# VectorE's modulation sums with 32x32 transpositions in place and folding products on TensorE

## The chip, the cores and the metric

The kernel runs on one core of one Trainium2 chip. The metric is the time of one execution on the device, in microseconds (us), taken as the median of several runs. Every matmul is in fp32 or in the fp32r form.

## What is computed

One layer of a hybrid diffusion backbone, for 128 context tokens and 128 latent tokens, width 2048. The shift, scale and gate vectors of three sublayers come from a modulation product, one row for the context and one for the latent tokens:

```
def modulation(cond, ada_w, ada_b):
    mod = jax.nn.silu(cond) @ ada_w + ada_b          # ada_w: 2048 x (9 * 2048)
    return jnp.split(mod[..., None, :], N_MOD, axis=-1)

xc = ffn_sublayer(xc, sh1, sc1, g1, ...)             # x + 0.5 * gate * swiglu(modulate(rms_norm(x)))
mq, mk, mv, ... = mixer_inputs(xc, sh2, sc2, ...)    # one 2048-wide input projection
...                                                  # mLSTM scan and windowed attention
xc = xc + g2 * merge_branches(...)                   # ends with the output projection w_out
xc = ffn_sublayer(xc, sh3, sc3, g3, ...)
```

The same layer runs on both groups of tokens, with the same weights. The change concerns how parts of `silu(cond) @ ada_w` are summed.

## The kernel before

**Units.** Both groups of tokens (2 x 128) share every weight. A weight tile of 256 x 512 is one unit: ScalarE rounds it (`w_hi`, L1354), VectorE makes the remainder (`w_lo`, L1810), and TensorE runs twelve matmuls of 512 columns on it (L702 to L704, three for each of two row blocks and two groups). `split(us + k + AHEAD)` prepares a unit three ahead of the one that TensorE is to work on; there are four slots for split weights, and ScalarE waits until TensorE has done the unit four before. There are 728 units in all. Each engine has a program of its own, written out by hand; semaphores tie them.

**The stages.** First FFN (a prologue, a loop over eight chunks of 512 hidden columns, and a last chunk), the input projection, the mLSTM and attention part, a merge, the output projection (`U_OUT`, four column chunks n of eight units k), the second FFN (in its loop two chunks a pass).

**The modulation.** The 36 chunks of 512 modulation columns are computed beside the units, in two ways. Half of them are products on TensorE. The other 18 are summed on VectorE: `products` (L1865) multiplies a 128x512 tile of `ada_w` by one scalar per partition and adds it to an accumulator of 2 x 512 columns per partition (`vec_acc`, `vec_m`, `vec_o`), 32 such steps for one chunk. What is left is a sum over the 128 partitions, and the result must lie with the columns on the partitions (`adacols`). For that, `vec_T` transposes the accumulator on TensorE, eight blocks of 128x128 into two PSUM banks (L648), and `sum_cols` reduces them on VectorE (L1838, 128x1024 to 128x8) and adds the bias (L1841).

**Where they stand.** In the first FFN's loop `vec_T` is called between units 6 and 7 of the eight output units (counted from 0), followed by the selection products (`ada_sel`, L656) and the transpositions of h (`h_transposes`, L779). L779 writes banks 4 and 5, and waits for the accumulation (L2015, semaphore `acc_done`) that VectorE makes at k = 5. In the last chunk `vec_T` comes after the first six units of the output part; before it, `ada_T` (L663) waits for VectorE's copy `ada_blk` (L1826). In the input projection it comes after the unit v = 11 of the second sixteen, in the output projection after units (n, k) = (1, 1) twice, (2, 1) and (3, 2), and in the second FFN after the second output unit of each odd chunk (`between`). The function `late_cols` calls `sum_cols` for these late chunks.

**Memory.** `cst` holds constants (identity, selection matrix, two triangles, two masks, cosines and sines); all tiles placed behind it in the same sequence, `hT_hi` and `hT_lo` among them, follow its width. The tiles from `cst` up to the slot of the accumulator `acc` take 8192 bytes per partition.

## Time and profile before

| | us |
|---|---|
| median of three runs | 2237.07 (2235.94 to 2237.38) |
| the profiled execution | 2237.59 |
| its span | 2235.6 |
| TensorE busy (PE) | 2207.9, 99% |
| VectorE busy (DVE) | 1607.7, 72% |
| ScalarE busy (ACT) | 937.0, 42% |

The times inside the profile are counted from the start of the span. Rows of a timeline give the start, the duration, the engine, the line, the operation with its operands and the number of instructions merged into the row; a bracket at the end tells how long the engine was idle before it, and what ended that. Durations of neighbouring matmuls overlap, so what a block of them costs is read from start to start. The stages lie at about 190 to 835 us (the loop and the last chunk of the first FFN), from 870 (input projection), from 1400 to 1495 (output projection) and from there on (second FFN).

### The profile page before, as it was taken

What the parts mean: (1) busy time and instruction counts of PE and PEld (TensorE: products, weight loads), DVE (VectorE), ACT (ScalarE), POOL (GpSimd) and SP (SyncE); (2) the same over time, 40 slices, a digit from 0 to 9 for tenths busy, and PEclk for the clock granted to TensorE, in tenths of its full rate; (3) what the DMA queues carried; (4) which work ended last, traced back from release to release, by engine and by line L of the source; (5) the groups of instructions that cost most, each with busy time, mean ns of one, the idle gap of its engine ahead of it and who ended that gap; (6) DMA issues with size and microseconds to landing.
All of it is one profiled execution on the core that took longest, in us unless ns stands there. A gap on an engine that the chain in (4) does not pass through costs nothing.

```text
span 2235.6 us, 28405 instructions
## 1 busy us (share of the span) xinstructions
PE 2207.9 (99%) x10498; PEld 1773.5 (79%) x10498; DVE 1607.7 (72%) x1859; ACT 937.0 (42%) x1100; POOL 64.5 (3%) x55
## 2 busy tenths in 40 slices
PE   6999999999999999999999999999999999999999
PEld 3567787878778778888888888888888888888887
DVE  3447888878887879746867888885567676776756
ACT  3333333333333336445544344454434444344443
POOL 0001000000000000000600000100000000000000
PEclk9999999999999999999999999999999999999999
DMA  9998898778887886644536776746675757557563
GB/s 361 385 367 292 287 322 300 278 277 291 315 283 281 281 271 208 217 161 160 190 109 234 260 258 234 270 157 207 224 241 190 263 188 262 188 188 262 188 226 131
DMA packets 273333, 548.15 MB, mean 245 GB/s; under 512 B 9014, under 2 KB 9418, under 8 KB 273008
## 3 DMA queue, kind: packets, MB, share of 16 engines
q1 hardware_dynamic: 212676, 423.69, 55.5%
q10 hardware_dynamic: 57484, 113.47, 14.1%
q0 software_dynamic: 3104, 10.05, 1.6%
q8 instruction: 46, 0.75, 0.1%
q14 instruction: 23, 0.19, 0.0%
HBM read 543.71 MB, written 3.46 MB: 245 GB/s over the span
## 4 chain that ended last, share of the span: by engine, by line
PE 96%; DVE 1%; DMA 1%; ACT 1%; issue 0%; SPq 0%; ACTq 0%
PE ps L702 30%; PE ps L704 29%; PE ps L703 29%; PE ps L639 1%; PE ps L624 1%; DMA ada_w_sb<-in_ada_w 1%; PE ps L779 1%; PE ps L648 1%; PE ps L689 0%; PE ps L1108 0%; PE ps L1176 0%; PE ps L656 0%; PE ps L1184 0%; DVE xm L1925 0%; DVE w_lo L1810 0%
## 5 line engine op out<-in xcount | busy, mean ns | idle before, releaser
L1354 ACT CAST w_hi<-raw_w 128x1024 fp32r<-128x1024 f32 x728 | 765.6, 1054 | 1171.3 <-PE ps L704 1128.7
L1810 DVE TENSOR_TENSOR w_lo<-raw_w,w_hi 128x1024 fp32r<-128x1024 f32 x728 | 897.4, 1236 | 433.5 <-ACT w_hi L1354 429.4
L702 PE MATMUL ps<-w_hi,xT_hi 128*128 128x512 f32 x2080 | 822.0, 395 | 5.8 <-DVE xT_lo L1893 4.5
L704 PE MATMUL ps<-w_hi,xT_lo 128*128 128x512 f32 x2080 | 811.1, 390 | 0.0
L703 PE MATMUL ps<-w_lo,xT_hi 128*128 128x512 f32 x2080 | 810.6, 390 | 0.0
L702 PEld LDWEIGHTS ps<-w_hi,xT_hi 128*128 128x128 f32 x2080 | 391.2, 188 | 111.0 <-issue 25.0
L704 PEld LDWEIGHTS ps<-w_hi,xT_lo 128*128 128x128 f32 x2080 | 390.9, 188 | 83.2
L703 PEld LDWEIGHTS ps<-w_lo,xT_hi 128*128 128x128 f32 x2080 | 391.3, 188 | 78.4
L1865 DVE SCALAR_TENSOR_TENSOR vec_acc<-ada_w_sb,ctile,vec_acc 128x512 f32<-128x512 f32 x420 | 299.2, 746 | 0.0
L702 PE MATMUL ps<-w_hi,hT_hi 128*128 128x512 f32 x704 | 276.2, 392 | 0.0
L704 PE MATMUL ps<-w_hi,hT_lo 128*128 128x512 f32 x704 | 274.2, 390 | 0.0
L703 PE MATMUL ps<-w_lo,hT_hi 128*128 128x512 f32 x704 | 273.9, 389 | 0.0
L704 PEld LDWEIGHTS ps<-w_hi,hT_lo 128*128 128x128 f32 x704 | 132.1, 188 | 27.7
L702 PEld LDWEIGHTS ps<-w_hi,hT_hi 128*128 128x128 f32 x704 | 132.2, 188 | 26.9 <-issue 0.2
L703 PEld LDWEIGHTS ps<-w_lo,hT_hi 128*128 128x128 f32 x704 | 132.3, 188 | 26.8
L2015 DVE TENSOR_TENSOR acc<-acc,ps 128x1024 f32<-128x1024 f32 x72 | 88.0, 1222 | 48.5 <-PE ps L704 48.5
L702 PE MATMUL ps<-w_hi,hcT_hi 128*128 128x512 f32 x128 | 50.1, 391 | 0.0
L704 PE MATMUL ps<-w_hi,hcT_lo 128*128 128x512 f32 x128 | 49.9, 390 | 0.0
L703 PE MATMUL ps<-w_lo,hcT_hi 128*128 128x512 f32 x128 | 49.8, 389 | 0.0
L1865 DVE SCALAR_TENSOR_TENSOR vec_m<-ada_m,ctile,vec_m 128x512 f32<-128x512 f32 x60 | 43.2, 746 | 0.0
L533 POOL DMA_DIRECT2D gate_dram<-gate_rows x3 | 1.6, 535 | 1414.8 <-DVE gate_rows L1821 1414.8
L1817 DVE TENSOR_TENSOR ada_rows_sb<-ps,ada_bias 128x512 f32<-128x512 f32 x18 | 12.2, 678 | 39.1 <-PE ps L624 39.1
(281 smaller groups left out, 1059.2 us busy)
## 6 DMA issues: line engine op xcount, KB each, us to landing
raw_w<-in_ffn_wi SPq DMA_DIRECT2D x176, 1024.0 KB, 5.2
ada_w_sb<-in_ada_w ACTq DMA_DIRECT2D x96, 1024.0 KB, 8.3
raw_w<-in_ffn_wo SPq DMA_DIRECT2D x88, 1024.0 KB, 5.3
raw_w<-in_w_in SPq DMA_DIRECT2D x68, 1024.0 KB, 5.4
ada_w_sb<-in_ada_w SPq DMA_DIRECT2D x30, 1024.0 KB, 13.0
raw_w<-in_w_out SPq DMA_DIRECT2D x16, 1024.0 KB, 5.3
ada_m<-in_ada_w ACTq DMA_DIRECT2D x12, 1024.0 KB, 5.2
raw_w<-in_w_proj_m SPq DMA_DIRECT2D x8, 1024.0 KB, 5.2
```

The lines of the kernel that those rows point to most:

```text
L624: mm = pe.matmul(ps[32 * j:32 * j + 32, 6, :], ctile[:, 4 * q + j, :], w[:, q, j, :], start=(q == 0), stop=(q == 3))
L639: mm = pe.matmul(ps[32 * j:32 * j + 32, 6, :], ctile[:, 4 * q + j, :], ada_w_sb[:, t, j, :], start=(q == 0), stop=(q == 3))
L648: mm = pe.transpose(ps[:, bank + g, b * P:(b + 1) * P], vec[:, g, b * P:(b + 1) * P], ident)
L702: pe.matmul(out, a_hi, w_hi[:, slot, kk, :], start=(first and kk == 0), stop=False)
L703: pe.matmul(out, a_hi, w_lo[:, slot, kk, :], start=False, stop=False)
L704: mm = pe.matmul(out, a_lo, w_hi[:, slot, kk, :], start=False, stop=(last and kk == 1))
L779: mm = pe.transpose(ps[:, 4 + b // 2, (b % 2) * TOK + g * P:(b % 2) * TOK + (g + 1) * P], h[:, g, b * P:(b + 1) * P], ident)
L1354: act.copy(w_hi[:, us % SPL, :, :], raw_w[:, slot, 2 * half:2 * half + 2, :]).then_inc(hi_ready, 1)
L1810: dve.tensor_tensor(w_lo[:, us % SPL, :, :], raw_w[:, slot, 2 * half:2 * half + 2, :], w_hi[:, us % SPL, :, :].bitcast(F32), ALU.subtract) ...
L1817: dve.tensor_tensor(ada_rows_sb[:], ps[:, 6, :], ada_bias[:, par, :], ALU.add).then_inc(ada_rows_done, 1)
L1865: ins = dve.scalar_tensor_tensor(acc[:, g, :], w, scale, acc[:, g, :], ALU.mult, ALU.add)
L2015: dve.tensor_tensor(acc[:, :, c], acc[:, :, c], ps[:, banks:banks + 2, :], ALU.add).then_inc(acc_done, 1)
```

## The change

The 18 sums over partitions are made differently. VectorE transposes the 128x1024 accumulator in place in blocks of 32x32 (`vec_fold`), waits for that, and reduces each run of 32 elements, which leaves 128x32 partial sums in `folded`. TensorE then adds the four groups of 32 partitions with a folding matrix: four products of 32 stationary and 8 moving columns (`vec_sum`) in place of eight transpositions. VectorE adds the bias straight from PSUM; the reduction after TensorE's part is gone. `vec_fold` is placed by hand: in the first FFN's loop at k = 5 of the output units, in its last chunk at e = 1, in the input projection at v = 26, in the output projection at (n, k) = (1, 0), (1, 2), (2, 0) and (3, 1), in the second FFN at k = 14 of the odd chunk's sixteen input units. The second sum of the output projection moves from (1, 1) to (1, 3) on TensorE. The masks are no longer constants: VectorE makes them from the triangles at v = 10, where ScalarE copied them; the constants grow by the folding matrix and lose the masks (816 to 592 columns), and the first part of them, which is loaded first, grows from 160 to 192 columns.

```diff
@@ -106,8 +106,8 @@
 
 
 
-C_ID, C_SEL, C_TRI, C_MASK, C_COS, C_SIN, C_TWO = 0, 128, 160, 416, 672, 736, 800
-C_W = 816
+C_ID, C_SEL, C_FOLD, C_TRI, C_COS, C_SIN, C_TWO = 0, 128, 160, 192, 448, 512, 576
+C_W = 592
 
 
 def shape_constants():
@@ -117,8 +117,7 @@
     c[:, C_ID:C_ID + P] = s == t
     c[:, C_TRI:C_TRI + P] = s <= t
     c[:, C_TRI + P:C_TRI + 2 * P] = s >= t
-    c[:, C_MASK:C_MASK + P] = np.where(s > t, 1e30, 0)
-    c[:, C_MASK + P:C_MASK + 2 * P] = np.where(s < t, 1e30, 0)
+    c[:, C_FOLD:C_FOLD + 32] = s % 32 == np.arange(32)[None, :]
     nf = HD // 4
     inv = np.float32(10000.0) ** (-np.arange(nf, dtype=np.float32) / np.float32(nf))
     for half, pos in enumerate((np.arange(P) // GRID_W, np.arange(P) % GRID_W)):
@@ -252,6 +251,7 @@
         row_sum = place("row_sum", [P, 2 * AH])
         neg_max = place("neg_max", [P, 2 * AH])
         biascol = place("biascol", [P, 4 * (NMOD * NCH - VCH2)])
+        folded = small[:, 16:48]
         hstat = small[:, 16:48].rearrange("p (a c) -> p a c", a=4)
 
         num = place("num", [P, NC, MV + 1], at=SCR)
@@ -297,7 +297,8 @@
         cols_ps, cond_silu, zeroed = sem("cols_ps"), sem("cond_silu"), sem("zeroed")
         ada_landed, bias_landed = sems("ada_landed", 4), sems("bias_landed", 2)
         ada_x_landed = sems("ada_x_landed", 2)
-        one_ready, mac_done, acc_T_done, acc_summed = sem("one_ready"), sem("mac_done"), sem("acc_T_done"), sem("acc_summed")
+        one_ready, mac_done = sem("one_ready"), sem("mac_done")
+        vec_turned, vec_folded, vec_summed = sem("vec_turned"), sem("vec_folded"), sem("vec_summed")
         ada_m_landed = sems("ada_m_landed", 2)
         ada_used, ada_rows_done = sem("ada_used"), sem("ada_rows_done")
         ada_sel_done, ada_cols_done = sem("ada_sel_done"), sem("ada_cols_done")
@@ -639,14 +640,14 @@
                     mm = pe.matmul(ps[32 * j:32 * j + 32, 6, :], ctile[:, 4 * q + j, :], ada_w_sb[:, t, j, :], start=(q == 0), stop=(q == 3))
                 mm.then_inc(ada_used, 1)
 
-            def vec_T(c, vec, done, bank):
+            def vec_sum(c, n, bank):
 
                 pe.wait_ge(ada_cols_done, c)
-                pe.wait_ge(mac_done, done)
-                for g in range(GROUPS):
-                    for b in range(4):
-                        mm = pe.transpose(ps[:, bank + g, b * P:(b + 1) * P], vec[:, g, b * P:(b + 1) * P], ident)
-                mm.then_inc(acc_T_done, 1)
+                pe.wait_ge(vec_folded, n)
+                for b in range(4):
+                    mm = pe.matmul(ps[32 * b:32 * b + 32, bank, 0:4 * GROUPS], cst[:, C_FOLD:C_FOLD + 32],
+                                   folded.rearrange("p (x b) -> p b x", b=4)[:, b, :], start=True, stop=True)
+                mm.then_inc(vec_summed, 1)
 
             def ada_sel(p, c):
 
@@ -909,7 +910,7 @@
                         if f == 0 and m == 1:
                             ada_T(i + 7)
                         if f == 0 and m == 2:
-                            vec_T(2 * i + 6, vec_acc, VEC_Z, 6)
+                            vec_sum(2 * i + 6, i - 1, 6)
                     if f == 0:
                         pe.wait_ge(ada_cols_done, VCH2)
                     for g in range(GROUPS):
@@ -934,7 +935,7 @@
                     with pe.Fori(2, FCH - 1) as i:
                         def sums():
                             pe.wait_ge(silu_done, i + 1)
-                            vec_T(2 * i + 5, vec_acc, (i - 1) * VEC, 0)
+                            vec_sum(2 * i + 5, i - 1, 0)
                             pe.wait_ge(gate_rows_ready, i - 1)
                             ada_sel(i + 7, 2 * i + 5)
 
@@ -943,7 +944,7 @@
                     with pe.Fori(1, 5) as t:
                         def between(n):
                             if n == 0:
-                                vec_T(t + 4 * G3 - 1, vec_acc, t * VEC + VEC_F2, 6)
+                                vec_sum(t + 4 * G3 - 1, t + FCH + 3, 6)
 
                         step(2 * t)
                         step(2 * t + 1, between)
@@ -1042,7 +1043,7 @@
                 if v == 7:
                     gate_rows_T()
                 if v == 11:
-                    vec_T(VCH2, vec_acc, VEC_M, 6)
+                    vec_sum(VCH2, FCH - 1, 6)
                 if v == 10:
                     scan_T()
                 if v == 12:
@@ -1086,7 +1087,7 @@
                 else:
                     pe.wait_ge(decays_ready, i - 1)
                 if i == 0:
-                    pe.wait_ge(masks_ready, 1)
+                    pe.wait_ge(masks_ready, 2)
                 for hd in range(MH):
                     out = ps[:, 4 + i % 2, hd * P:(hd + 1) * P]
                     pe.matmul(out, ident_r[:], mask_r[:, d, :], start=True, stop=False)
@@ -1323,12 +1324,13 @@
                         pe.wait_ge(mixT_lo_ready, min(k + 2, 8))
                     unit(U_OUT + 8 * n + k, 0, xT_hi, xT_lo, 2 * k, 2 * (n % 2), k == 0, k == 7)
                     if n == 1 and k == 1:
-                        vec_T(VCH, vec_m[0], VEC_O, 4)
-                        vec_T(VCH, vec_m[1], VEC_O, 6)
+                        vec_sum(VCH, FCH, 4)
+                    if n == 1 and k == 3:
+                        vec_sum(VCH + 1, FCH + 1, 6)
                     if n == 2 and k == 1:
-                        vec_T(VCH + 2, vec_m[2], VEC_O, 4)
+                        vec_sum(VCH + 2, FCH + 2, 4)
                     if n == 3 and k == 2:
-                        vec_T(VCH + 3, vec_o, VEC_F2, 4)
+                        vec_sum(VCH + 3, FCH + 3, 4)
             for g in range(GROUPS):
                 for k in range(4, 8):
                     mm = unit(U_OUT + 24 + k, 0, xT_hi, xT_lo, 2 * k, 2, False, k == 7, groups=(g,))
@@ -1628,8 +1630,7 @@
                     ada_tile(VCH, v - 1, v - 1)
                 if v == 10:
                     act.wait_ge(consts_landed, 16)
-                    act.copy(ident_r[:], cst[:, C_ID:C_ID + P])
-                    act.copy(mask_r[:].rearrange("p d t -> p (d t)"), cst[:, C_MASK:C_MASK + 2 * P]).then_inc(masks_ready, 1)
+                    act.copy(ident_r[:], cst[:, C_ID:C_ID + P]).then_inc(masks_ready, 1)
                 if v == 18:
                     act.wait_ge(absf_ready, 1)
                     chain(act.activation(exp_negm[:], absf[:], ACT.Exp, scale=-1.0))
@@ -1831,14 +1832,19 @@
                 dve.tensor_copy(adacols[:, bass.ds(4 * at, 4), :],
                                 ps[:, 7, P:2 * P].rearrange("p (b x) -> p b x", x=32)[:, :, 0:GROUPS]).then_inc(ada_cols_done, 1)
 
+            def vec_fold(n, vec, done):
+
+                dve.wait_ge(mac_done, done)
+                flat = vec[:].rearrange("p g n -> p (g n)")
+                dve.transpose(flat, flat).then_inc(vec_turned, 1)
+                dve.wait_ge(vec_turned, n)
+                dve.tensor_reduce(folded, flat.rearrange("p (x k) -> p x k", k=32), AX.X, ALU.add).then_inc(vec_folded, 1)
+
             def sum_cols(c, n, bank, bias, done=None):
 
                 dve.wait_ge(ada_cols_done, c if done is None else done)
-                dve.wait_ge(acc_T_done, n)
-                dve.tensor_reduce(small[:, 48:56], ps[:, bank:bank + 2, :].rearrange("p g (b k) -> p (g b) k", k=P), AX.X, ALU.add
-                                  ).then_inc(acc_summed, 1)
-                dve.wait_ge(acc_summed, n)
-                dve.tensor_tensor(adacols[:, bass.ds(4 * c, 4), :], small[:, 48:56].rearrange("p (g b) -> p b g", g=GROUPS),
+                dve.wait_ge(vec_summed, n)
+                dve.tensor_tensor(adacols[:, bass.ds(4 * c, 4), :], ps[:, bank, 0:4 * GROUPS].rearrange("p (g b) -> p b g", g=GROUPS),
                                   bias.unsqueeze(2).to_broadcast([P, 4, GROUPS]),
                                   ALU.add).then_inc(ada_cols_done, 1)
 
@@ -1982,6 +1988,8 @@
                             d_products(i, k)
                         if g3:
                             g3_products(g3[1], g3[2], g3[0] + k)
+                            if g3[0] and k == 14:
+                                vec_fold(g3[1] - 4 * G3 + FCH + 4, vec_acc, g3[2] + VEC)
                         if k == 15:
                             dve.wait_ge(units_done, us + ux + 16)
                             dve.wait_ge(silu_done, FCH * f + i + 1)
@@ -1992,6 +2000,8 @@
                 def ffn_out(j, us, ux, ada=None, g3=None):
 
                     for k in range(8):
+                        if ada is not None and k == 5:
+                            vec_fold(j, vec_acc, j * VEC)
                         if ada is not None and k == 7:
                             sum_cols(2 * j + 7, j, 0, biascol1[:, bass.ds(8 * j - 8, 4)])
                         split(us + k + AHEAD, ux)
@@ -2048,6 +2058,8 @@
                                 gates_copy((G1,), i - 1)
                                 ada_rows(i + 7, 1, 16 * i + 48)
                                 d_products(i, 16)
+                            if e == 1:
+                                vec_fold(i - 1, vec_acc, VEC_Z)
                             if e == 3:
                                 ada_blk(i + 7)
                             if e == 4:
@@ -2240,6 +2252,12 @@
                 if v:
                     split(U_IN + v + AHEAD, 0)
                 products(MACS_Z, 0, VCH2, VEC_Z, v)
+                if v == 10:
+                    dve.wait_ge(consts_landed, 16)
+                    dve.tensor_scalar(mask_r[:].rearrange("p d t -> p (d t)"), cst[:, C_TRI:C_TRI + 2 * P], -1e30, 1e30,
+                                      ALU.mult, ALU.add).then_inc(masks_ready, 1)
+                if v == 26:
+                    vec_fold(FCH - 1, vec_acc, VEC_M)
                 if v == 28:
                     late_cols(VCH2, 6, VCH)
                 if v == 16:
@@ -2483,10 +2501,19 @@
                     split(U_OUT + 8 * n + k + AHEAD, 0)
                     products(MACS_O, 0, VCH2, VEC_O, 8 * n + k, [ada_w_sb[:, q % 2, :, :] for q in range(4)], [ada_landed[q % 2] for q in range(4)],
                              [(400, 400)[q % 2] + 16 * (1 + q // 2) for q in range(4)], vec_o)
-                    if n == 1 and k in (2, 3):
-                        late_cols(VCH - 2 + k, 2 * k, VCH - 1 + k)
+                    if n == 1 and k == 0:
+                        vec_fold(FCH, vec_m[0], VEC_O)
+                    if n == 1 and k == 2:
+                        late_cols(VCH, 4, VCH + 1)
+                        vec_fold(FCH + 1, vec_m[1], VEC_O)
+                    if n == 1 and k == 4:
+                        late_cols(VCH + 1, 6, VCH + 2)
+                    if n == 2 and k == 0:
+                        vec_fold(FCH + 2, vec_m[2], VEC_O)
                     if n == 2 and k == 2:
                         late_cols(VCH + 2, 4, VCH + 3)
+                    if n == 3 and k == 1:
+                        vec_fold(FCH + 3, vec_o, VEC_F2)
                     if n == 3 and k == 3:
                         late_cols(VCH + 3, 4, VCH2)
                 c = slice(n * CH, (n + 1) * CH)
```

## Rows read from the trace of the kernel before

**Rows 1.** The page: busy lines, the chain that ended last, the costliest groups.
```profile
PE 2207.9 (99%) x10498; PEld 1773.5 (79%) x10498; DVE 1607.7 (72%) x1859; ACT 937.0 (42%) x1100; POOL 64.5 (3%) x55
...
PE 96%; DVE 1%; DMA 1%; ACT 1%; issue 0%; SPq 0%; ACTq 0%
...
L702 PE MATMUL ps<-w_hi,xT_hi 128*128 128x512 f32 x2080 | 822.0, 395 | 5.8 <-DVE xT_lo L1893 4.5
...
L702 PE MATMUL ps<-w_hi,hT_hi 128*128 128x512 f32 x704 | 276.2, 392 | 0.0
```

**Rows 2.** Timeline of TensorE, output projection, n = 3: transpositions standing alone.
```profile
1476.85 0.39 PE L704 MATMUL ps<-w_hi,xT_lo 128*128 128x512 f32 x1
1477.08 1.03 PE L648 MATMUL ps<-cst,vec_o 128*128 128x128 f32 x8
1477.87 0.48 PE L702 MATMUL ps<-w_hi,xT_hi 128*128 128x512 f32 x1
1478.18 0.40 PE L703 MATMUL ps<-w_lo,xT_hi 128*128 128x512 f32 x1
```

**Rows 3.** Timeline of TensorE, first FFN's loop, one of eight passes.
```profile
261.02 1.03 PE L648 MATMUL ps<-cst,vec_acc 128*128 128x128 f32 x8
...
262.34 1.09 PE L779 MATMUL ps<-cst,h 128*128 128x128 f32 x8
```

**Rows 4.** Timeline of TensorE, three stretches: small products.
```profile
205.24 1.92 PE L639 MATMUL ps<-ada_w_sb,ctile 128*32 128x512 f32 x16
...
823.58 0.43 PE L656 MATMUL ps<-ada_rows_sb,cst 128*32 128x128 f32 x8
823.94 0.50 PE L702 MATMUL ps<-w_hi,hT_hi 128*128 128x512 f32 x1
824.28 0.40 PE L703 MATMUL ps<-w_lo,hT_hi 128*128 128x512 f32 x1
...
933.29 0.61 PE L1007 MATMUL ps<-lf,cst 128*128 128x8 f32 x4
933.76 0.48 PE L702 MATMUL ps<-w_hi,xT_hi 128*128 128x512 f32 x1
```

**Rows 5.** Groups of VectorE by line and shape: busy, mean ns | idle before.
```profile
L1838 DVE TENSOR_REDUCE small<-ps 128x8 f32<-128x1024 f32 x18 | 22.0, 1222 | 9.7 <-PE ps L648 9.7
...
L1862 DVE TENSOR_SCALAR vec_acc<-ada_w_sb,ctile 128x512 f32<-128x512 f32 x28 | 12.6, 481 | 0.0
...
L1841 DVE TENSOR_TENSOR adacols<-small,biascol 128x8 f32 x12 | 2.0, 168 | 3.1 <-DVE small L1838 3.1
...
L1841 DVE TENSOR_TENSOR adacols<-small,biascol 128x8 f32<-128x8 f32 x6 | 1.0, 167 | 0.2
```

**Rows 6.** Timeline of all engines, last chunk of the first FFN.
```profile
822.65 2.47 DVE L1810 TENSOR_TENSOR w_lo<-raw_w,w_hi 128x1024 fp32r<-128x1024 f32 x2
...
829.27 0.28 DVE L1826 COPY ada_rows_sb<-ps 128x128 f32<-128x128 f32 x1
...
829.61 0.33 PE L663 MATMUL ps<-cst,ada_rows_sb 128*128 128x128 f32 x1
```

**Rows 7.** Timeline of VectorE, first FFN's loop, the pass of rows 3.
```profile
255.42 1.41 DVE L1865 SCALAR_TENSOR_TENSOR vec_acc<-ada_w_sb,ctile,vec_acc 128x512 f32<-128x512 f32 x2
...
258.59 1.22 DVE L2015 TENSOR_TENSOR acc<-acc,ps 128x1024 f32<-128x1024 f32 x1 [0.49 <-PE ps L704]
```

**Rows 8.** Timeline of all engines, input projection.
```profile
952.59 2.35 DVE L1810 TENSOR_TENSOR w_lo<-raw_w,w_hi 128x1024 fp32r<-128x1024 f32 x2
...
954.00 1.04 PE L648 MATMUL ps<-cst,vec_acc 128*128 128x128 f32 x8
```

**Rows 9.** Timeline of all engines, output projection, n = 1 and n = 3.
```profile
1427.32 0.74 DVE L1865 SCALAR_TENSOR_TENSOR vec_o<-ada_w_sb,ctile,vec_o 128x512 f32<-128x512 f32 x1
...
1428.15 1.04 PE L648 MATMUL ps<-cst,vec_acc 128*128 128x128 f32 x8
...
1474.86 2.35 DVE L1810 TENSOR_TENSOR w_lo<-raw_w,w_hi 128x1024 fp32r<-128x1024 f32 x2
```

## The prediction

> **What bounds the kernel now.** I read the page's busy lines first: TensorE is busy for 99% of the span [rows 1], and the chain of work that ended last is TensorE for 96% of it [rows 1]. The waits of TensorE come next: its largest group of matmuls, 2080 of them, has 5.8 us of idle time ahead of it in the whole span, 4.5 of them put down to VectorE's xT_lo [rows 1]. So a microsecond taken off TensorE's queue comes off the time, and a wait put into that queue is paid in full. Then I read the timelines around the places the change touches, to see what TensorE's own work costs there and how early VectorE, which is busy 72% of the time, gets to the same place.
>
> **TensorE: what the transpositions cost now.** There are 18 vector sums of eight transpositions, 144 in all: eight in the loop of the first FFN, and ten that stand alone (one after that loop, one in the input projection, four in the output projection, four in the second FFN). The page's means (0.27 us for one) overlap each other, so I go from start to start.
> - Alone: the eight start at 1477.08 and the following matmul at 1477.87; that matmul then takes 0.31 us to the next start, against 0.23 in the steady stream (1476.85 to 1477.08) [rows 2]. So 0.79 + 0.08 = 0.87 us each.
> - In the loop: they start at 261.02, and behind them and the four selection products (L656) the eight transpositions of h (L779) at 262.34 [rows 3]. So 1.32 us to L779.
>
> **TensorE: what the four folding products cost.** No row has a 32-column stationary operand with 8 moving columns. The nearest is L656: four fp32 products with the same 32-column form, 128 moving columns, recorded as eight instructions. They take 823.58 to 823.94, 0.36 us, and the next matmul 0.34 instead of 0.23, another 0.11 [rows 4]. With 512 moving columns (L639) sixteen of them take some 1.9 us, 0.12 each, against 0.045 each at 128 [rows 4]; the straight line through the two gives 0.02 each at 8 columns, 0.17 for the block. Bounds 0.17 and 0.36; I take 0.25, since short products rarely follow such a line to its end. A far bound is L1007, 8 moving columns but a 128-column stationary operand: 933.29 to 933.76 for four, 0.12 each [rows 4], 0.94 for eight. It is a rival below.
> The Trainium skill ("TensorE: Matmul & The Clock Gate", Part 1) says that starts never come closer than about 25 ns however few the columns. By it the block would be an estimated 0.20 us and the sum 0.5 us lower than with my 0.25; no run here shows the floor yet.
>
> So alone: 0.87 - (0.25 + 0.11) = 0.51 us saved, ten times, 5.1 us, if nothing is waited for.
>
> **VectorE: the price of a fold.** Removed is one reduction of 128x1024 out of PSUM, 1.22 us [rows 5]; added are a transposition of 128x1024 in place and the same reduction out of SBUF. No row has a transposition. VectorE's plain operations of this size, one operand or two, take 1.22 [rows 5, 7]; below, the one-operand 128x512 form takes 0.48 [rows 5], so 0.96 at most if the transposition ran so; above, two passes would be 2.44. I take 1.22, the row of its size and kind (one operand, one result). The reduction waits for the transposition through a semaphore: the same kind of dependent pair shows 0.2 us idle for six outside the loops, some 0.04 each, and 3.1 for twelve inside them, 0.26 each, with an address computed in between that the fold's reduction lacks [rows 5]; I take 0.04 outside and 0.15 inside. From a VectorE end to the TensorE start it releases, 0.06 us (829.27 + 0.28 to 829.61) [rows 6]. A fold outside the loops therefore needs 1.22 + 0.04 + 1.22 + 0.06 = 2.54 us from its start to TensorE's. The added 22 us of VectorE time (18 x 1.22) are covered where VectorE has slack; what matters is that the fold now lies **ahead** of TensorE's sum, where before the only VectorE step, the reduction, lay behind it.
> The Trainium skill ("Vector Engine (DVE) Microarchitecture Reference", 3.8) says that the 32x32 transposition sustains one element a cycle per lane; by it the price is that of my row, and the sum stands. Against it, "VectorE: DVE Perf Modes" (the three transpose paths) gives 311 ns for 128x128; eight of those are an estimated 2.5 us. That would be the two-pass rival.
>
> **First FFN's loop, eight passes.** The fold stands behind the last product (255.42 + 1.41, so 256.87) [rows 7]. Transposition to 258.09, 0.15, reduction; starts of this size follow each other by 1.14 (two w_lo lie within 2.35) [rows 8]: w_lo at 259.38, the accumulation L2015 at 260.52 (now 258.59), done 261.74. TensorE's sum wants the fold at 261.02 and has it (259.5). But L779 overwrites the banks that this accumulation reads and waits for it: 261.80. TensorE by itself would be there at 261.02 + 0.25 + 0.36 = 261.63. So L779 starts at 261.80 instead of 262.34: 0.54 saved, eight times 4.3 us, and no more however cheap the products are. Behind it, w_lo keeps over two units of lead, and VectorE recovers because the reduction after L779 is gone.
>
> **The places where the fold comes late.**
> - Input projection: the fold goes between the two w_lo that start at 952.59, so at 953.73, ready 956.27; TensorE arrives at 954.00 [rows 8]: wait 2.27.
> - Output projection, n=1: after the product of 1427.32 (ends 1428.06), so 1428.10, ready 1430.64; TensorE arrives at 1428.15 [rows 9]: 2.49. The n=2 place repeats it (product 0.8 us ahead of the transpositions): 2.49.
> - n=1, second sum: TensorE is back after 0.36 and two units (24 matmuls of 0.227, 5.44) at 1436.44; VectorE has w_lo, two products, w_lo and the small sum in between and is ready at 1436.74: 0.30.
> - n=3: between the two w_lo that start at 1474.86, so 1476.00, ready 1478.54, against 1477.08 [rows 2, 9]: 1.46.
> - End of the first FFN: the fold goes between the two w_lo from 822.65, so 823.79; reduction 825.05, w_lo 826.19, hT_lo 827.33 (wanted at 829.7), w_lo 828.46, copy L1826 829.60 to 829.88 instead of 829.27 + 0.28; TensorE's L663 waits for it and moves from 829.61 to 829.94 [rows 6]: 0.33.
> - Second FFN: the fold lies ahead of the product h, which waits for unit 16 of the pass; TensorE's sum lies two more units, 5.4 us, behind that unit. No wait.
> Sum 9.34 us. They are not given back: behind each of them TensorE has no other wait that the delay could fill.
>
> **The rest**, at nothing: the masks move from ScalarE to VectorE (some 0.4 us, in a stretch where VectorE waits for w_hi several times before anyone needs them); the first constants are 32 columns wider, behind them TensorE waits for other transfers anyway; PSUM instead of SBUF for the final small sum. Uncovered, the three together would be under 1 us. All tiles behind the constants move down by 896 bytes, so hT leaves the 256-byte phase it shares with w_hi; no row compares two phases.
>
> **Sum:** -5.1 - 4.3 + 9.3 = -0.1 us. The profiled execution took 2237.59 us for a span of 2235.6; the median is 2237.07. Forecast on the median: 2237 us.
> With the transposition at 0.96: five places 1.3, the second sum 0.3 and the loop 8 x 0.17 less, 3.0 in all, 2234. With the block at 0.17 or 0.36, 0.8 less or 1.1 more. With 0.26 for the dependent wait in the loop, 0.9 more.
>
> **Rivals.**
> - *Two passes.* The transposition takes 2.44. Each of the five places pays 1.22 more, the second sum too, and L779 in the loop waits 1.22 more eight times: 14 x 1.22 = 17.1, so 2254. For it: no row excludes it. Against: the other plain operations of this size cost 1.22.
> - *The products don't fold cheaply.* At 0.94 for the block: ten times 0.69 and eight times 0.52 more, 11.1, so 2248. Against: L656 in the 32-column form takes 0.045 an instruction.
> - *The moved tiles.* If hT's new phase cost each of the 2112 matmuls with hT as much as the mean of L702 differs between its operands (395 and 392 ns) [rows 1], 3 ns, that is 6.3 us: 2243.
> - *The other side: no waits.* If VectorE reached the folds 2.5 us earlier than its rows say, the 9.3 vanish and the loop saves 0.71 a pass: -10.8, so 2226. It decides from the point where each fold starts 2.5 us before TensorE's arrival; the products in front of the folds stand against it [rows 8, 9].
>
> **Chances.** Near nothing 0.57, two passes 0.13, dear products 0.08, moved tiles 0.07, something else that costs 0.02, no waits 0.13. The measurement tells 0.2%, 4.5 us, from no change: faster 0.13, same 0.57, slower 0.30. Range 2230 to 2255: it takes in the three dear rivals and leaves out most of the cheap one; the forecast's own range is 2233 to 2241.
>
> **What would show it.** On VectorE one transposition of 1.22 us before each reduction; TensorE waits for that reduction at four places by 1.5 to 2.5 us; L779 waits in the loop for L2015, some 0.2 us each; from the start of the folding products to the next matmul 0.25. Wrong would be: a transposition of another length (fourteen-fold in the sum), another spacing of matmuls with hT than 0.23, or TensorE without waits at the output projection.

## The result, and the profile after

The changed kernel takes 2247.06 us (median of 5 runs, 2245.70 to 2250.35), the kernel before 2237.07. The ratio is 1.0046 with a 95% interval of 1.0035 to 1.0056: 10 us slower, where no change was forecast; it lies in the range on record (2230 to 2255), toward its dear end. The profiled execution took 2245.7 us for a span of 2243.8.

The page of the changed kernel, its busy lines, the chain that ended last and the costliest groups (its L703 to L705 are L702 to L704 before):

```profile
PE 2209.5 (98%) x10498; PEld 1761.6 (79%) x10498; DVE 1626.0 (72%) x1878; ACT 935.4 (42%) x1099; POOL 64.5 (3%) x55
...
PE 95%; DVE 3%; DMA 1%; ACT 1%; issue 0%; SPq 0%; ACTq 0%; DVEq 0%
...
L703 PE MATMUL ps<-w_hi,xT_hi 128*128 128x512 f32 x2080 | 823.2, 396 | 5.8 <-DVE xT_lo L1899 4.6
...
L703 PE MATMUL ps<-w_hi,hT_hi 128*128 128x512 f32 x704 | 279.7, 397 | 0.0
L705 PE MATMUL ps<-w_hi,hT_lo 128*128 128x512 f32 x704 | 277.4, 394 | 0.0
L704 PE MATMUL ps<-w_lo,hT_hi 128*128 128x512 f32 x704 | 277.4, 394 | 0.0
```

Against [rows 1], VectorE has moved into the chain that ended last (1% to 3%): from each of the waits that were forecast the chain goes back through VectorE's work, so the 2% (some 45 us) are not the length of the waits. The other change wasn't forecast: the mean of L703 with hT is 397 ns instead of 392, while with xT it hardly moves (396, before 395). Nothing in the edit touches the program of these matmuls.

What TensorE waits for in the changed kernel (us in total, times, longest):

```profile
PE ps L957 <- DMA colrows<-in_norm_ffn_w: 9.4, 1, 9.4
PE ps L648 <- DVE small L1841: 8.2, 4, 2.3
PE ps L703 <- DVE xT_lo L1899: 4.6, 3, 3.3
```

The second line is the new one. Its first wait in the output projection, on TensorE and then on VectorE (timelines):

```profile
1426.75 0.39 PE L705 MATMUL ps<-w_hi,xT_lo 128*128 128x512 f32 x1
1429.45 0.25 PE L648 MATMUL ps<-small,cst 128*32 128x8 f32 x8 [2.31 <-DVE small L1841]
1429.63 0.50 PE L703 MATMUL ps<-w_hi,xT_hi 128*128 128x512 f32 x1
1429.96 0.40 PE L704 MATMUL ps<-w_lo,xT_hi 128*128 128x512 f32 x1
...
1430.45 0.63 PE L703 MATMUL ps<-w_hi,xT_hi 128*128 128x512 f32 x1
1430.88 0.63 PE L704 MATMUL ps<-w_lo,xT_hi 128*128 128x512 f32 x1
...
1433.84 0.40 PE L705 MATMUL ps<-w_hi,xT_lo 128*128 128x512 f32 x1
1434.08 0.39 PE L703 MATMUL ps<-w_hi,xT_hi 128*128 128x512 f32 x1
```

```profile
1426.81 1.24 DVE L1839 STREAM_TRANSPOSE vec_acc<-vec_acc 128x1024 f32<-128x1024 f32 x1
1428.09 1.22 DVE L1841 TENSOR_REDUCE small<-vec_acc 128x32 f32<-128x1024 f32 x1
```

The fold is 1.24 + 0.04 + 1.22 + the way to TensorE, and TensorE stands still for it. Behind the wait there is a second thing to see: the matmuls from 1430.45 to 1433.84, eight of them, start 0.42 us apart and not 0.23. The windows of TensorE (length, busy and instructions, granted clock, DMA share, GB/s) show the clock:

```profile
1425.00:1430.00 5.00, 2.69 (x20) 1.00 0.49 157
1430.00:1435.00 5.00, 5.00 (x16) 0.66 0.28 78
1435.00:1440.00 5.00, 5.00 (x30) 1.00 1.00 361
```

The mean of 0.66 is a stretch at the lower of the two levels, 1.2 GHz. Eight starts take 3.39 us there (1430.45 to 1433.84) instead of 8 x 0.227 = 1.82: some 1.6 us, 1.7 with its edges. In the kernel before, no window between 1400 and 1440 is below 1.00. The equal wait at 1456.03 has no such stretch behind it in this execution.

TensorE in the loop, the pass of [rows 3], changed kernel:

```profile
254.74 0.39 PE L705 MATMUL ps<-w_hi,hT_lo 128*128 128x512 f32 x1
...
260.31 0.39 PE L705 MATMUL ps<-w_hi,hT_lo 128*128 128x512 f32 x1
260.62 0.25 PE L648 MATMUL ps<-small,cst 128*32 128x8 f32 x8
260.71 0.40 PE L657 MATMUL ps<-ada_rows_sb,cst 128*32 128x128 f32 x8
261.09 1.06 PE L780 MATMUL ps<-cst,h 128*128 128x128 f32 x8
```

From the first of these rows to the second lie 24 matmuls, 5.57 us, 0.232 each. The steady stream was 0.227. And L780 starts with no wait on VectorE, where one of 0.2 us was forecast.

### The profile page after: what moved, and what is told of

It reads as the page before. It is cut to its first block, busy times and chain, and to the rows that moved or that the text cites. A ratio compares the mean times of both kernels' runs of the same rounds, so it can differ in the third digit from the quotient of the medians.

```text
span 2243.8 us, 28431 instructions
## 1 busy us (share of the span) xinstructions
PE 2209.5 (98%) x10498; PEld 1761.6 (79%) x10498; DVE 1626.0 (72%) x1878; ACT 935.4 (42%) x1099; POOL 64.5 (3%) x55
## 4 chain that ended last, share of the span: by engine, by line
PE 95%; DVE 3%; DMA 1%; ACT 1%; issue 0%; SPq 0%; ACTq 0%; DVEq 0%
PE ps L703 29%; PE ps L705 29%; PE ps L704 29%; PE ps L640 1%; PE ps L625 1%; DMA ada_w_sb<-in_ada_w 1%; PE ps L780 1%; DVE w_lo L1811 1%; PE ps L690 0%; PE ps L1109 0%; DVE vec_o L1871 0%; PE ps L1177 0%; ACT w_hi L1356 0%; PE ps L1185 0%; DVE xm L1931 0%
## 5 line engine op out<-in xcount | busy, mean ns | idle before, releaser
L703 PE MATMUL ps<-w_hi,xT_hi 128*128 128x512 f32 x2080 | 823.2, 396 | 5.8 <-DVE xT_lo L1899 4.6
L705 PE MATMUL ps<-w_hi,xT_lo 128*128 128x512 f32 x2080 | 811.9, 390 | 0.0
L704 PE MATMUL ps<-w_lo,xT_hi 128*128 128x512 f32 x2080 | 811.2, 390 | 0.0
L703 PEld LDWEIGHTS ps<-w_hi,xT_hi 128*128 128x128 f32 x2080 | 391.5, 188 | 111.3 <-issue 25.0
L705 PEld LDWEIGHTS ps<-w_hi,xT_lo 128*128 128x128 f32 x2080 | 391.3, 188 | 83.3
L704 PEld LDWEIGHTS ps<-w_lo,xT_hi 128*128 128x128 f32 x2080 | 391.8, 188 | 79.2
L703 PE MATMUL ps<-w_hi,hT_hi 128*128 128x512 f32 x704 | 279.7, 397 | 0.0
L705 PE MATMUL ps<-w_hi,hT_lo 128*128 128x512 f32 x704 | 277.4, 394 | 0.0
L704 PE MATMUL ps<-w_lo,hT_hi 128*128 128x512 f32 x704 | 277.4, 394 | 0.0
L705 PEld LDWEIGHTS ps<-w_hi,hT_lo 128*128 128x128 f32 x704 | 132.6, 188 | 30.8
L704 PEld LDWEIGHTS ps<-w_lo,hT_hi 128*128 128x128 f32 x704 | 132.7, 188 | 29.7
L703 PEld LDWEIGHTS ps<-w_hi,hT_hi 128*128 128x128 f32 x704 | 132.6, 188 | 29.9 <-issue 0.2
L703 PE MATMUL ps<-w_hi,hcT_hi 128*128 128x512 f32 x128 | 50.1, 391 | 0.0
L705 PE MATMUL ps<-w_hi,hcT_lo 128*128 128x512 f32 x128 | 49.8, 389 | 0.0
L704 PE MATMUL ps<-w_lo,hcT_hi 128*128 128x512 f32 x128 | 49.8, 389 | 0.0
```

The source lines that it names most:

```text
L703: pe.matmul(out, a_hi, w_hi[:, slot, kk, :], start=(first and kk == 0), stop=False)
L704: pe.matmul(out, a_hi, w_lo[:, slot, kk, :], start=False, stop=False)
L705: mm = pe.matmul(out, a_lo, w_hi[:, slot, kk, :], start=False, stop=(last and kk == 1))
```

## The experiments

The theory from this profile had three parts: hT's new offset costs 5 ns in each of 2112 matmuls (10.6 us), the four waits cost 8.2 and now and then a slower clock, and the savings are about as forecast. Its rivals: the masks on VectorE or the moved tables cost it, or the folding itself slows the stream around it. "Spacing" below is the mean start-to-start time of consecutive matmuls with hT (2044 pairs) and with xT (some 6000) in a run's trace, steps above 300 ns left out. The kernel before was timed again beside each batch of runs, on the same chip: 2237.59 us beside pad128, pad896 and the two masks runs, 2237.81 beside later_pad, later, pad64 and shift_w, 2237.39 beside one_wait, add_first, pad160 and pad192. Offsets are in bytes modulo 256. Before, `w_hi`, `w_lo`, `hT` and `xT` all lie at the same one, counted here as 128; in the changed kernel hT lies at 0. Only the differences matter below.

The profile leaves the numbers out of tiles' names, so its hT also takes in 192 matmuls with `hT2_hi` and `hT2_lo` (eight units in the last chunk of each FFN), which lie at w's offset in every kernel. Told apart by their place in the program, the spacing is 232.4 ns with hT and 228.2 with hT2 in the changed kernel, 227.0 and 226.8 in the kernel before. So 1920 matmuls, not 2112, pay for the offset, 5.4 ns each, 10.4 us; 5.0 ns is the mean of the whole group, and 5.0 x 2112 = 10.6 us the same sum by it.

**pad128.** Changed kernel, with 128 unused bytes behind the constants, so that hT is back at the offset of w_hi.

```
         cst = place("cst", [P, C_W])
+        top[0] += 128
```

> The changed kernel with 128 bytes left empty behind the constants, so that hT_hi and hT_lo lie at the same offset modulo 256 as w_hi again, and at other addresses than before the change. Theory A (hT's offset): the spacing of matmuls with hT falls from 232 ns to 227, 5.1 ns x 2112 = 10.7 us less than the changed kernel, so 2236 to 2237. Theory B (the folds' waits and the clock cost the 10 us, the offset nothing): 2247, spacing irrelevant.

**pad896.** The same line with 896: every tile behind the constants is back at its address of before.

> The changed kernel with 896 bytes left empty behind the constants: every tile lies where it lay before the change. Theory A: the same as with 128 bytes, 2236 to 2237, waits of TensorE for the reduction still 8.2 us. Theory B: 2247. If something else in the addresses matters than the offset modulo 256, this one and the one with 128 bytes differ.

Measured: pad128 2240.09 us, ratio 1.0013 [1.0004, 1.0022]; pad896 2240.76, 1.0011 [1.0002, 1.0020]. Spacing with hT 227.0 ns in both, 232.0 in the changed kernel; with xT 227.2 or 227.3 in all three. So 128 bytes give back 7 of the 10 us, and the other 768 nothing. The group with hT on the page of pad128:

```profile
L704 PE MATMUL ps<-w_hi,hT_hi 128*128 128x512 f32 x704 | 276.3, 392 | 0.0
```

The loop of pad128, the same pass (TensorE):

```profile
255.03 0.39 PE L706 MATMUL ps<-w_hi,hT_lo 128*128 128x512 f32 x1
...
260.47 0.39 PE L706 MATMUL ps<-w_hi,hT_lo 128*128 128x512 f32 x1
260.79 0.25 PE L649 MATMUL ps<-small,cst 128*32 128x8 f32 x8
260.88 0.40 PE L658 MATMUL ps<-ada_rows_sb,cst 128*32 128x128 f32 x8
261.46 1.06 PE L781 MATMUL ps<-cst,h 128*128 128x128 f32 x8 [0.18 <-DVE acc L2026]
```

24 matmuls in 5.44 us, 0.227 each; and now the wait that was forecast is there, 0.18 us a pass. The slower matmuls had hidden it. What remains of pad128 against the kernel before is the waits and what the clock adds to them, less the savings. Its profile has two stretches at 1.2 GHz, one of them in a window that was at full clock in the changed kernel:

```profile
1425.00:1430.00 5.00, 2.81 (x16) 0.80 0.64 210
1430.00:1435.00 5.00, 5.00 (x27) 0.86 0.65 199
...
1455.00:1460.00 5.00, 5.00 (x16) 0.66 0.44 138
```

So the 7.0 us from the changed kernel to pad128 is 10.6, less 1.4 for the loop's wait that comes back (8 x 0.18), less 1.7 for a second slow stretch in the profiled execution: 7.5.

**masks and masks_pad.** The kernel before with only the masks moved to VectorE (the constants 1024 bytes narrower, all tiles at the same offset modulo 256), and that with the line `top[0] += 128`, which puts hT at 0.

```
-C_W = 816
+C_ID, C_SEL, C_TRI, C_COS, C_SIN, C_TWO = 0, 128, 160, 416, 480, 544
+C_W = 560
...
-                    act.copy(mask_r[:].rearrange("p d t -> p (d t)"), cst[:, C_MASK:C_MASK + 2 * P]).then_inc(masks_ready, 1)
...
+                    dve.tensor_scalar(mask_r[:].rearrange("p d t -> p (d t)"), cst[:, C_TRI:C_TRI + 2 * P], -1e30, 1e30,
+                                      ALU.mult, ALU.add).then_inc(masks_ready, 1)
```

> The kernel before with the masks' part of the change alone: VectorE makes them, constants 1024 bytes narrower (so no tile's offset modulo 256 changes). Both theories: no change, 2237 within 1 us. If the masks on VectorE cost something that was put at nothing, it shows here.

> The same as the masks alone, with 128 bytes left empty behind the constants: transpositions on TensorE as before the change, hT off w_hi's offset modulo 256. Theory A: 10.7 us slower, 2248, spacing of matmuls with hT 232 ns. Theory B: 2237, spacing 227.

Measured: masks 2237.87 us, 1.0000 [0.9991, 1.0009]; masks_pad 2247.76, 1.0044 [1.0030, 1.0058], 9.9 more. The masks cost nothing, and hT's offset alone, with no fold in the kernel, costs what the whole change cost. The two pages, masks first:

```profile
L700 PE MATMUL ps<-w_hi,hT_hi 128*128 128x512 f32 x704 | 276.2, 392 | 0.0
```

```profile
L701 PE MATMUL ps<-w_hi,hT_hi 128*128 128x512 f32 x704 | 279.5, 397 | 0.0
```

Spacing with hT 227.0 and 232.0: 5.0 x 2112 = 10.6 us against the 9.9 measured by the medians (10.4 less 0.1 by the count of matmuls at the end of this section).

**later_pad and later.** The waits. later_pad is pad896 with the sums of the input and output projection one or two units later on TensorE (the diff), VectorE's bias sums `late_cols` one or two units later in the output projection (with the second fold of n = 1), and the fold in the last chunk of the first FFN at e = 3 instead of 1. later is that without the padding.

```
-                if v == 11:
+                if v == 12:
                     vec_sum(VCH2, FCH - 1, 6)
...
-                    if n == 1 and k == 1:
+                    if n == 1 and k == 2:
                         vec_sum(VCH, FCH, 4)
-                    if n == 1 and k == 3:
+                    if n == 1 and k == 5:
                         vec_sum(VCH + 1, FCH + 1, 6)
-                    if n == 2 and k == 1:
+                    if n == 2 and k == 2:
                         vec_sum(VCH + 2, FCH + 2, 4)
-                    if n == 3 and k == 2:
+                    if n == 3 and k == 3:
                         vec_sum(VCH + 3, FCH + 3, 4)
```

> The changed kernel with every tile where it lay before the change (896 bytes left empty) and the sums of the late places moved one unit or more behind their folds: input projection from after unit 11 to after unit 12, output projection (1,1), (1,3), (2,1), (3,2) to (1,2), (1,5), (2,2), (3,3), VectorE's steps behind them likewise, and in the last chunk of the first FFN the fold from e = 1 to e = 3. Theory A, with waits and clock as the rest of the account: the 8.2 us of waits go, and with them the two stretches of 3.4 us at the lower clock (3.4 us), so 2240.8 - 11.6 = 2229, faster than before the change by 8. Rival (the waits only move elsewhere): 2237 or more.

> The same moved sums with the changed kernel's own addresses (hT off w_hi's offset modulo 256). Theory A: 10.7 us above the one with the empty bytes, 2239 to 2240; that would be the changed kernel less its waits and its one stretch at the lower clock in the profiled run.

Measured: later_pad 2229.79 us, 0.9966 [0.9952, 0.9979]; later 2237.08, 0.9998 [0.9988, 1.0007]. So the change is worth having once nothing waits and hT is not moved. Waits of TensorE in later_pad:

```profile
PE ps L781 <- DVE acc L2026: 1.4, 8, 0.2
...
PE ps L649 <- DVE small L1842: 0.7, 1, 0.7
```

8.2 us of waiting in four places has become 0.7 in one, and in the output projection all windows are at 1.00. But in the input projection, where the fold's wait is gone, a new one stands a unit later, for VectorE's `decay`:

```profile
950.57 0.61 PE L1027 MATMUL ps<-mcol,cst 128*128 128x4 f32 x4 [0.70 <-DVE decay L2243]
```

So 6.8 us of waits are gone and not 7.5. From pad896 to later_pad the medians fall by 11.0 us: 6.8 of waits, 3.4 of the clock (pad896 has two slow stretches in its profile), and 0.3 at the end of the first FFN, where the fold at e = 3 no longer delays the copy. The padding is worth 7.3 us here by the medians and 9.8 by the spans of the profiled executions (2235.4 and 2225.6). Worked out it is 10.6 - 1.4, since the wait for acc is gone in later: 9.2; by the count of matmuls below it is 9.3. From the changed kernel to later, both with hT at 0, it is 10.0 us by the medians and 8.6 by the count of matmuls: 6.8 of waits, 1.7 of the clock.

**one_wait.** later_pad with the input projection's sum back at v = 11, a single wait of 2.2 us.

```
-                if v == 12:
+                if v == 11:
```

> The version with the sums moved and every tile where it lay before the change, but the sum of the input projection back after unit 11: one wait of TensorE of 2.3 us for the reduction. If a wait costs its length alone: 2.3 us above the version with all sums moved, 2232. If it also brings a stretch of 3.4 us at half the clock in some executions: 1.7 us more in those, a median up to 2234, and two groups of times.

Measured: 2230.62 us, 0.9971 [0.9959, 0.9982]; the wait is there (2.9 in two places instead of 0.7 in one), with no slow stretch behind it. The medians' difference of 0.8 us doesn't resolve it, since the intervals overlap. The traces do: every matmul behind the input projection starts 1.5 us later than in later_pad. That is the 2.2 of the wait less the 0.7 of later_pad's wait for `decay`, which is gone here. So this wait cost its length and hid another.

**add_first.** later_pad, with VectorE's accumulation ahead of w_lo at k = 5 in the loop, to take out the wait of 0.2 us a pass that decided the forecast's term for the loop.

```
-                        split(us + k + AHEAD, ux)
+                        add_first = ada is not None and k == 5
+                        if not add_first:
+                            split(us + k + AHEAD, ux)
...
+                        if add_first:
+                            split(us + k + AHEAD, ux)
```

> The version with the sums moved, and in the first FFN's loop VectorE's accumulation at k = 5 ahead of w_lo instead of behind it. The wait of the transpositions of h for it, 0.2 us in each of eight passes, goes: 1.4 us less than 2230, about 2228. Rival (w_lo comes too late in its place and TensorE waits for it): no less than 2230.

Measured: 2227.92 us, 0.9952 [0.9939, 0.9966], the fastest of all, 9.5 us below the 2237.39 of the kernel before beside it. The line of acc is gone from TensorE's waits. The step from later_pad is 1.9 us in the medians, with overlapping intervals, and 1.4 by the waits; by the starts of the same matmuls it is 1.8. The start of L658 and that of L781 lie 0.25 us closer in a pass than in later_pad (0.33 for 0.58), though the wait was 0.17:

```profile
261.83 0.41 PE L658 MATMUL ps<-ada_rows_sb,cst 128*32 128x128 f32 x8
262.16 1.09 PE L781 MATMUL ps<-cst,h 128*128 128x128 f32 x8
```

**shift_w.** Is it where hT lies, or where it lies against the weights? Changed kernel with w_hi and w_lo (the moving operands) moved by 128 to offset 0 as well: hT and w agree, xT doesn't.

```
         xT_lo = place("xT_lo", [P, KD, TOK], F32R)
+        top[0] += 128
         raw_w = place("raw_w", [P, RAW, 4, CH])
...
         w_lo = place("w_lo", [P, SPL, 2, CH], F32R)
         cst = place("cst", [P, C_W])
+        top[0] += 128
```

> The changed kernel with raw_w, w_hi and w_lo moved up by 128 bytes and hT moved to the same offset as they (both 0 modulo 256; before the change both 128), while xT stays at 128. If what counts is stationary against moving operand: hT at 227 ns, but the 6240 matmuls with xT at 232, 6240 x 5 = 31 us, less 10.7 for hT, so about 2268. If what counts is the stationary operand's own offset (128 good, 0 bad): xT 227, hT 232, 2247. If w's own: both the same.

Measured: 2271.4 us, 1.0148 [1.0132, 1.0164]. Spacing with hT 227.1, with xT 232.4. The page:

```profile
L705 PE MATMUL ps<-w_hi,xT_hi 128*128 128x512 f32 x2080 | 833.5, 401 | 6.0 <-DVE xT_lo L1901 4.5
...
L705 PE MATMUL ps<-w_hi,hT_hi 128*128 128x512 f32 x704 | 276.4, 393 | 0.0
```

5.2 ns x 6240 = 32 us; pad128, where w lies at xT's offset too, is 31.3 below. xT itself has not moved: what counts is the stationary operand's offset against that of the moving one.

**pad64, pad160, pad192.** pad128 with 64, 160 and 192 in place of 128: hT at 64 below, 32 above and 64 above w's offset.

> The changed kernel with 64 bytes left empty behind the constants: hT lies 64 bytes off w_hi's offset modulo 256, neither the changed kernel's 128 nor 0. If any offset but 0 costs the same: spacing 232 ns, 2247. If the cost belongs to 128 alone: 227 ns, 2240.

> The changed kernel with 160 bytes left empty behind the constants: hT 32 bytes above w_hi's offset modulo 256. If the cost grows with the distance from w_hi's offset (0 at 0, 1.9 ns at 64, 5.0 at 128): spacing 227 to 228 ns, 2240 to 2242. If 0 isn't the best offset, the spacing falls below 227.

> The changed kernel with 192 bytes left empty: hT 64 bytes above w_hi's offset, where the one with 64 bytes lay 64 below. If only the distance counts: spacing 228.9 ns, 2244. If the direction counts: another value.

Measured, with the spacing with hT: pad64 2243.98 us, 1.0029 [1.0018, 1.0039], 228.9 ns; pad160 2250.74, 1.0057 [1.0041, 1.0072], 232.6; pad192 2248.99, 1.0050 [1.0035, 1.0065], 232.9. The expectation that a small distance costs little is wrong: 32 bytes above cost more than 128. And pad64 is uneven. Its page:

```profile
L704 PE MATMUL ps<-w_hi,hT_hi 128*128 128x512 f32 x704 | 278.0, 395 | 0.0
L705 PE MATMUL ps<-w_lo,hT_hi 128*128 128x512 f32 x704 | 276.7, 393 | 0.0
L706 PE MATMUL ps<-w_hi,hT_lo 128*128 128x512 f32 x704 | 273.9, 389 | 0.0
```

By these means with hT_hi 3 to 4 ns more than at equal offsets, with hT_lo nothing, though both lie at the same offset modulo 256. The offsets measured are too few for a rule, and why these differ stays open. What is shown is that equal offsets gave 227.0 or 227.1 ns with hT in eight kernels, with the old sums and the new, and every unequal one tried gave a larger mean.

**The same matmuls in every trace.** All kernels run the same 8736 matmuls of 512 columns (728 units of twelve) in the same order, so their starts can be set against each other one by one. Before the 289th the executions differ by up to 3 us whatever the kernel: the first starts at 38.7 to 41.5 us, and up to some 131 us TensorE waits for transfers of `ada_w`. Why they differ there wasn't pursued. Behind it the traces agree closely:

| | the 289th starts | the last | between them | against before | slow stretches between |
|---|---|---|---|---|---|
| before | 144.14 | 2231.03 | 2086.9 | | 0 |
| changed | 142.58 | 2239.15 | 2096.6 | +9.7 | 1 |
| pad128 | 143.83 | 2233.16 | 2089.3 | +2.4 | 2 |
| pad896 | 145.19 | 2234.51 | 2089.3 | +2.4 | 2 |
| masks | 144.66 | 2231.66 | 2087.0 | +0.1 | 0 |
| masks_pad | 144.04 | 2241.32 | 2097.3 | +10.4 | 0 |
| later | 142.79 | 2230.78 | 2088.0 | +1.1 | 0 |
| later_pad | 142.30 | 2220.96 | 2078.7 | -8.2 | 0 |
| one_wait | 142.26 | 2222.45 | 2080.2 | -6.7 | 0 |
| add_first | 144.78 | 2221.63 | 2076.9 | -10.0 | 0 |

## Why the prediction failed, step by step

**The step that failed** is the last sentence of "The rest": that all tiles behind the constants move down by 896 bytes, that hT so leaves the offset it shares with w_hi, and that no row compares two phases, priced at nothing. It costs 10.6 us. The mechanism stood in the text, among the rivals, with a chance of 0.07 and a price of 3 ns a matmul taken from the difference between two operands in [rows 1]; both of those operands lay at w_hi's offset, so that row could not bound it. The measured price is 5.0 ns on the mean of the group (masks against masks_pad), 5.4 on each of the 1920 matmuls that pay it. An unknown cost that is paid some 2000 times in a kernel whose TensorE is busy for 99% of the span deserves the widest bound of the list, not the narrowest. The source held a hint too: `hT2_hi` and `hcT_hi` are placed with `(W_AT - SCR) % 256`, which puts them at w's offset. That the rival of dear products had 2248, 1 us from the measured time, is chance: its mechanism is out, as the rows below show.

**The second term left out** is the clock. The waits were priced at their length. In the profiled executions of the changed kernel and of pad128, pad896, pad64, pad160, pad192 and shift_w one or two of the waits have 3.4 us at 1.2 GHz behind them, 1.7 us each on top of their length. later, later_pad, add_first and one_wait have none in the middle of the span. How many the other executions have isn't known; the mean granted clock is 0.996 to 0.998 in those of the changed kernel and 0.998 to 0.999 in those of later. In the trace of before TensorE has no wait of this size in the output projection, but it has one of 3.35 us near the start, and the matmuls behind it start 0.43 us apart until 44.8 us:

```profile
40.39 0.80 PE L702 MATMUL ps<-w_hi,xT_hi 128*128 128x512 f32 x1 [3.35 <-DVE xT_lo L1893]
40.98 0.63 PE L703 MATMUL ps<-w_lo,xT_hi 128*128 128x512 f32 x1
41.41 0.63 PE L704 MATMUL ps<-w_hi,xT_lo 128*128 128x512 f32 x1
```

The window from 40 to 45 us has a granted clock of 0.52. So the trace that the forecast was made from did show that a wait can cost more than its length, for a longer wait than the four that were priced.

**Right, with sizes.**
- The fold: 1.24 + 0.04 + 1.22 (forecast 1.22 + 0.04 + 1.22). The two-pass rival is out: the group of transpositions has a mean of 1.24 us. The Trainium skill ("Vector Engine (DVE) Microarchitecture Reference", 3.8), one element a cycle per lane, agrees with it. The estimate of 2.5 us from 311 ns for 128x128, which the Trainium skill ("VectorE: DVE Perf Modes", the three transpose paths) gives for bf16, doesn't.
- The waits: 2.20, 2.31, 2.31 and 1.39, 8.2 in all, for 2.27, 2.49, 2.49 and 1.46. The second sum at n = 1 does not wait at all (0.30 forecast), and the end of the first FFN costs 0.35 (0.33), read from where the same matmul starts in pad128 and in the kernel before.
- The folding products alone, changed kernel, end of the first FFN (TensorE):

```profile
832.28 0.39 PE L705 MATMUL ps<-w_hi,hT_lo 128*128 128x512 f32 x1
832.60 0.25 PE L648 MATMUL ps<-small,cst 128*32 128x8 f32 x8
832.78 0.50 PE L703 MATMUL ps<-w_hi,hT_hi 128*128 128x512 f32 x1
833.12 0.39 PE L704 MATMUL ps<-w_lo,hT_hi 128*128 128x512 f32 x1
```

  0.84 us from 832.28 to 833.12 for what would be two steps of 0.23 without them: 0.38, where the transpositions cost 0.87. So 0.49 saved each (0.51 forecast). The block itself takes 0.18 (0.25 taken, 0.17 the lower bound), but 0.09 more lies in front of it, a step that the forecast didn't have. The dear products are out. The Trainium skill ("TensorE: Matmul & The Clock Gate", Part 1), starts no closer than about 25 ns, would make the block an estimated 0.20: near the 0.18, though the eight in the loop show only 0.09 to the start of L657 (260.62 to 260.71), which a floor of that size does not allow if the rows' starts are taken as exact.
- The loop: in pad128 L781 waits 0.18 us a pass for the accumulation, as forecast, and a pass is 0.60 shorter (0.54), by where the same matmuls start in pad128 and in the kernel before. In the changed kernel the slow matmuls bring TensorE there later and the wait vanishes, so a pass saves 0.78 (by its rows: 0.47 from the products to L780 instead of 1.32 [rows 3], less 0.08 in front of them, 0.77).
- The masks: nothing (masks, 1.0000).

**The sum as it came out**, changed kernel against before: hT 10.6 + waits 8.2 + clock 1.7 + end of the first FFN 0.4 - loop 8 x 0.78 = 6.2 - alone 10 x 0.49 = 4.9: +9.8 us. Measured 10.0 by the medians and 9.7 by the count of matmuls; the spans of the two profiled executions differ by 8.2 only, since the changed kernel's was 1.6 us ahead at the 289th matmul. With hT in place (pad128) the forecast's own terms give 8.2 + 0.4 - 4.8 - 4.9 = -1.1, where -0.1 stands on record; with two slow stretches, 3.4, that is +2.3. pad128 measured +2.5 by the medians and +2.4 by the count of matmuls. What was priced was priced to within 1 us in all, and what was left at nothing made the result.

## What to carry to other kernels

When an edit resizes one table, list every tile that moves and check whether a matmul's stationary operand keeps its offset modulo 256 against its moving one: here 128 bytes cost 10.6 us, about as much as the edit saves on TensorE (6.2 + 4.9), and one line of padding gives it back. A step on a second engine that used to lie behind TensorE's work and now lies ahead of it needs its whole length as a lead; move the consumer by a unit (one constant here) before judging the idea: the same sums, one or two units later and with hT in place, are 8 us faster than before, and 9.5 with the accumulation moved. A saving and a wait on the same path hide each other, so undo suspected costs one at a time and in both orders.

## What the runs showed of the hardware that was not expected

- The start-to-start time of 512-column fp32r matmuls depends on where the stationary operand lies against the moving one in SBUF: 227.0 ns at equal offsets modulo 256 (0, 768 and 1024 bytes away from the first placement); at 128 apart 232.0 with hT moved and 232.4 with w moved; 232.6 at 32 above; 232.9 at 64 above; 228.9 at 64 below, where only the matmuls with hT_hi are slower. The values with hT moved are means of the whole group, hT2 included. Why the direction counts is open.
- After a wait of 2.1 to 2.3 us amid dense work TensorE's granted clock can fall to 1.2 GHz for 3.4 us, and after the next equal wait not. Which of the waits it follows differed between kernels that are alike there: 1430 to 1434 alone in the changed kernel, from 1428 and from 1455 in pad128, from 1429 and from 1457 in pad896, from 954 and from 1432 in pad64 (0.94 and 0.71 in its windows from 950 to 960, 0.73 from 1430 to 1435). No run was made to tell what picks it.
- A 32x32 transposition of 128x1024 fp32 in place on VectorE takes 1.24 us, next to the 1.21 to 1.23 of plain operations of that size in the same trace.
